# A mixture-of-experts kernel on one core: first expert's rows by one-hot weights, a short main list, and an overflow list made by GpSimd

## What is computed

```python
logits = h @ w_router + b_router                # 512 x 32
top_val, top_idx = top_k(logits, 4)
gates = softmax(top_val)
order = argsort(top_idx.reshape(-1)); tok = order // 4
xs = h[tok]                                     # rows sorted by expert
hgu = ragged_dot(xs, w_gate_up, group_sizes) + b_gate_up[e_sorted]
act = clamped_swiglu(hgu)
out = ragged_dot(act, w_down, group_sizes) + b_down[e_sorted]
moe = segment_sum(out * gates[order], tok)
h = layernorm(ALPHA * h + moe)
```

## Time and profile before

| what | value |
|---|---|
| median of 3 runs | 2309.36 us (2308.25 to 2310.8) |
| the profiled execution | 2309.27 us |
| its span | 2307.4 us |
| mean granted clock of TensorE | 0.985 |
| busy: TensorE, VectorE, ScalarE, GpSimd | 2228.9, 1664.4, 1220.2, 339.9 us |

### The profile page before, as it was taken

The page is one execution under the profiler, slowest core; times in us unless marked ns, Lnnn a source line. Parts: engine busy times, 40 slices in busy tenths (PEclk is TensorE's granted clock), DMA queues, the critical chain, the costliest instruction groups (busy, mean ns, idle before and its releaser), DMA issues.

```text
span 2307.4 us, 29229 instructions
## 1 busy us (share of the span) xinstructions
PE 2228.9 (97%) x10480; PEld 1821.2 (79%) x10480; DVE 1664.4 (72%) x1618; ACT 1220.2 (53%) x1228; POOL 339.9 (15%) x274
## 2 busy tenths in 40 slices
PE   8999959999999999999999999889999999999998
PEld 4668847888888888888888888778777778888886
DVE  2647678999999999999999999882557536433434
ACT  2135336767767777677677777643435532322320
POOL 4042111311111211111112111100130010000000
PEclk9999959999999999999999999999999999999999
DMA  7030149999999999999999999862221232223220
GB/s 276 3 103 1 58 162 357 397 393 381 379 392 377 392 378 379 394 373 386 387 379 393 379 378 396 302 238 83 84 86 37 110 119 100 84 99 110 77 105 37
DMA packets 141524, 551.96 MB, mean 239 GB/s; under 512 B 11552, under 2 KB 12704, under 8 KB 124368
## 3 DMA queue, kind: packets, MB, share of 16 engines
q1 hardware_dynamic: 128240, 507.29, 57.1%
q0 software_dynamic: 10736, 38.93, 6.5%
q10 hardware_dynamic: 2480, 4.80, 0.6%
HBM read 523.18 MB, written 25.69 MB: 238 GB/s over the span
## 4 chain that ended last, share of the span: by engine, by line
PE 79%; DVE 4%; issue 1%; ACT 1%; DMA 0%; DVEq 0%; ACTq 0%
PE PS L389 76%; PE PS L706 1%; PE PS L700 1%; ACT act L1732 1%; DVE ring_parts L2321 1%; DVE small L2408 1%; DVE act L1849 0%; DVE st L1822 0%; PE PS L979 0%; DVE act L1854 0%; DVE act L2435 0%; DMA act<-h_d,tl_c 0%; DVE act L2425 0%; PE PS L880 0%; DVE act L2519 0%
## 5 line engine op out<-in xcount | busy, mean ns | idle before, releaser
L389 PE MATMUL PS<-act_parts 128*128 128x512 f32 x3404 | 1073.2, 394 | 17.3 <-DVE act_parts L2189 8.1
L2034 DVE TENSOR_TENSOR low<-ring,act_parts 128x2048 fp32r<-128x2048 f32 x380 | 851.1, 2293 | 32.6 <-ACT act_parts L1492 32.5
L389 PEld LDWEIGHTS PS<-act_parts 128*128 128x128 f32 x3404 | 641.1, 190 | 150.6 <-issue 17.8
L1492 ACT ACTIVATE act_parts<-ring 128x2048 fp32r<-128x2048 f32 x384 | 707.7, 1914 | 16.4 <-PE PS L389 7.9
L389 PE MATMUL PS<-low,act_parts 128*128 128x512 f32 x1584 | 618.7, 391 | 0.0
L389 PE MATMUL PS<-act_parts,ring_parts 128*128 128x512 f32 (+1 forms) x1344 | 397.1, 382 | 0.0
L389 PEld LDWEIGHTS PS<-low,act_parts 128*128 128x128 f32 x1584 | 298.6, 189 | 60.6
L389 PEld LDWEIGHTS PS<-act_parts,ring_parts 128*128 128x128 f32 x1344 | 248.1, 188 | 58.6 <-issue 10.7
L389 PE MATMUL PS<-ring_parts,act_parts 128*128 128x512 f32 x1088 | 261.7, 393 | 3.1 <-DVE act_parts L2485 2.1
L389 PE MATMUL PS<-ring_parts 128*128 128x512 f32 (+1 forms) x672 | 255.5, 380 | 0.0
L389 PEld LDWEIGHTS PS<-ring_parts,act_parts 128*128 128x128 f32 x1088 | 204.9, 189 | 49.1 <-issue 3.5
(11 more groups left out here) (264 smaller groups left out, 1707.1 us busy)
## 6 DMA issues: line engine op xcount, KB each, us to landing
ring<-w_gate_up SPq DMA_DIRECT2D x264, 1024.0 KB, 8.7
ring<-w_down SPq DMA_DIRECT2D x132, 1024.0 KB, 7.9
ring<-w_ff SPq DMA_DIRECT2D x16, 2048.0 KB, 7.8
ring<-w_in SPq DMA_DIRECT2D x12, 2048.0 KB, 8.1
ring<-w_o SPq DMA_DIRECT2D x1, 4096.0 KB, 24.2
ring<-w_out SPq DMA_DIRECT2D x2, 2048.0 KB, 7.7
acc_d<-ring POOLq DMA_DIRECT2D x5, 512.0 KB, 3.2
act<-x SPq DMA_DIRECT2D x4, 512.0 KB, 5.7
```

The source lines that it names most:

```text
L389: return eng.matmul(o, lhsT, rhs, start=first, stop=last, **kw)
L1492: A_(W1hi[c % CS], W1[c], ACT.Copy).then_inc(sem["high"], 1)
L2034: tt(W1lo[c], W1[c], W1hi[c % CS].bitcast(F32), ALU.subtract).then_inc(sem["low"], 1)
```

## The change

1. **First expert's rows.** As soon as the rank matrix of a token tile is there (now one bank each), VectorE copies it and compares the rank in expert 0 with 0 to 127: a one-hot `OH0`. TensorE multiplies it as weights with h, which lies in SBUF, eight fp32 products of 512 columns (`first_rows`); ScalarE copies the two banks to where a gather would have put the rows. There is no gather for item 0, and item 1's is the first.
2. **Main list.** Only ranks below 128 count, so the list needs no positions: one-hots of the rank, and a table of 64 columns (token number by ScalarE, `token_hot`; gate by VectorE), 16 fp32 products 128x64. It names the tiles of experts 0 to 30.
3. **Overflow.** What is beyond, and the last expert, go to a list of 17 columns. GpSimd makes it while the first items run: counts, prefixes (`count_past`), picks by one-hot (`pick`, twice), and four tables (`over_table`), one for each token tile, of 12 operations. TensorE multiplies them in items 2 and 3, behind chunk 6, two tables each (`list_over`), and VectorE writes the two halves out at the end of items 2 and 3 (`halve_over`, `list_over`), the counts in item 1 (`name_over`).
4. **First gate-up** (`first_gate_up`): bias at its second half first and at the end of the first; the base products two behind each of the chunks 4 to 7, in two banks; the split of gates and down bias by ScalarE and GpSimd. Gate sums by VectorE from the table of the list. Items 1 to 3 are written out, the loop starts at 4.
5. **Order elsewhere.** ScalarE makes three chunks' high parts ahead of the row copies and the others behind; the memset of the bias rows waits for the one-hots; (0,10) and (0,11) are loaded behind item 1's eight chunks; `chunk_low(1, 0)` stands ahead of the last two bases.

The diff, cut to what the steps speak of:

```diff
+            def first_rows(hf):
+                take(hf, "rows_out", hf + 1)
+                for t in range(NT):
+                    if hf == 0:
+                        eng.wait_ge(*past("first_hot", 2 * t + 2))
+                    ins = mm(PS[:, hf, :], OH0[:, t, :], H1[:, t, hf * 512:(hf + 1) * 512], t == 0, t == NT - 1)
+                    if hf == 0 and t == 0:
+                        ranks(3)
+                ins.then_inc(put("rows_psum", hf), 1)
...
+            def list_over(t):
+                eng.wait_ge(*past("over_made", t + 1))
+                for j in range(TOPK):
+                    ins = mm(PS[:, 4, 0:2 * OVER], over_hot[t % 2][:, j, :], over_tok[t % 2][:, j, :],
+                             t % 2 + j == 0, t % 2 + j == TOPK)
...
-            eng.wait_ge(sem["rows_in"], 16)
-            turn_rows()
...
+                        if isinstance(i, int) and i > 1 and c == 6:
+                            eng.wait_ge(sem["down_free"], i)
+                            list_over(2 * i - 4)
+                            list_over(2 * i - 3)
...
+            first_gate_up()
             turn_gated(0, 0)
             turn_gated(0, 1)
-            with eng.Fori(1, LAST) as i:
+            gate_up(1)
+            for b in (4, 5):
+                eng.wait_ge(*free[b])
+            down(1)
+            gate_up(2)
+            eng.wait_ge(*past("over_halved", 1))
+            down(2)
+            gate_up(3)
+            eng.wait_ge(*past("over_summed", 1))
+            down(3)
+            with eng.Fori(4, LAST) as i:
...
+            def first_hot(t):
+                eng.wait_ge(*past("rank_psum", t + 1))
+                eng.tensor_copy(R2[:, t, :], bank_of("rank_psum", t + 1)[:, 0:E]).then_inc(
+                    signal("first_hot"), 1)
+                eng.wait_ge(*latest("first_hot"))
+                ts(OH0[:, t, :], iotas, R2[:, t, 0:1], Mm[:, t, 0:1], ALU.is_equal, ALU.mult).then_inc(
+                    signal("first_hot"), 1)
...
+            for c in range(4, 6):
                 chunk_low(0, c)
             swiglu(0, 0, again=False)
-            for n in range(4, 2 * NT):
+            chunk_low(0, 6)
+            base(0)
+            base(1)
+            chunk_low(0, 7)
+            for n in range(2, 6):
                 base(n)
...
+            chunk_low(1, 0)
+            base(6)
+            base(7)
             swiglu(0, 1, again=False)
             rows_low(1)
-            with eng.Fori(1, LAST) as i:
+            item(1, name_over)
+            item(2, halve_over)
+            item(3, list_over)
+            with eng.Fori(4, LAST) as i:
                 item(i)
...
+            def pick(x, to):
+
+                for t in range(NT):
+                    chosen = slice(TOPK * t, TOPK * (t + 1))
+                    tt(picked[:, chosen, :], OH[:, chosen, :], x[:, t:t + 1, :].to_broadcast([P, TOPK, E]),
+                       ALU.mult).then_inc(signal("pool_step"), 1)
+                eng.wait_ge(*latest("pool_step"))
+                n = E // 2
+                while n > 1:
+                    tt(picked[:, :, 0:n], picked[:, :, 0:n], picked[:, :, n:2 * n], ALU.add).then_inc(
+                        signal("pool_step"), 1)
...
+            def over_table(t):
+
+                if t > 1:
+                    eng.wait_ge(*past("over_psum", t - 1))
+                hot, tok = over_hot[t % 2], over_tok[t % 2]
+                for k in range(TOPK):
+                    n = TOPK * t + k
+                    ts(hot[:, k, :], iotas, slotf[:, n:n + 1], None, ALU.is_equal).then_inc(signal("pool_step"), 1)
+                    ts(tok[:, k, 0:OVER], iotas[:, LAST:ITEMS + 1], itemf[:, n:n + 1], TOKID1[:, t:t + 1],
+                       ALU.is_equal, ALU.mult).then_inc(signal("pool_step"), 1)
...
+            pick(beyond, itemf)
+            next_select(1)
+            pick(more_past, slotf)
+            over_table(0)
+            eng.wait_ge(*past("places_listed", 1))
             eng.wait_ge(*past("sums_begun", 80))
-            with eng.Fori(2, LAST) as i:
+            next_rows(2)
+            add_product(2)
+            over_table(1)
+            next_select(2)
+            over_table(2)
+            next_rows(3)
+            add_product(3)
+            over_table(3)
+            next_select(3)
+            eng.wait_ge(*past("over_listed", 3))
+            with eng.Fori(4, LAST) as i:
                 item(i)
```

More of the change, by code:

```diff
@@ L652, in _ @@
+            ranks(0)
+            cur[0] = 0
             turn_tile(NT - 1)
-            ranks(0)
+            ranks(1)
             router(NT - 1)
-            ranks(1)
             ranks(2)
-            ranks(3)
-            for t in range(NT):
-                ins = mm(PS[0:E, rank_bank, 256:257], Mm[:, t, :], ones[:, 0:1], t == 0, t == NT - 1)
-            ins.then_inc(put("rank_psum", rank_bank), 1)
-            eng.wait_ge(*past("extras", 2))
-            b = next_bank()
-            eng.wait_ge(*free[b])
@@ L730, in base, with bias @@
                     eng.wait_ge(*past("bd_low", 1))
-                if n >= 4:
-                    eng.wait_ge(*past("based", n - 3))
-                b = (4, 5, 2, 3, 4, 5, 6, 7)[n]
+                b = 4 + n % 2
+                take(b, "based", n + 1)
                 mm(PS[:, b, :], GT[:, t, :], bd3[:, hf * 512:(hf + 1) * 512]).then_inc(put("base_psum", b), 1)
-            def gate_up(i, again=True):
-                if not again:
-                    for n in range(4):
-                        base(n)
+            def bias(hh, first):
+                for n in range(2):
+                    cols = slice((2 * hh + n) * 512, (2 * hh + n + 1) * 512)
+                    ins = mm(PS[:, 2 * hh + n, :], sel, bias2[:, cols], first, not first)
+                return ins
@@ new lines, in first_gate_up @@
+            def first_gate_up():
+                for b in range(4):
+                    eng.wait_ge(*free[b])
+                eng.wait_ge(sem["xT_low"], 1)
+                for c in range(8):
+                    hh = c // 4
+                    if c == 4:
+                        eng.wait_ge(*past("bias_lo", 2))
+                        bias(1, True)
+                    eng.wait_ge(sem["low"], count_high(0, c))
+                    for kk in range(2):
+                        k = 2 * (c % 4) + kk
+                        ins = bf3(2 * hh, (xThi[:, k, :], xTlo[:, k, :]), c, kk, hh == 0 and k == 0, hh == 1 and k == KD - 1)
+                    if c == 3:
+                        eng.wait_ge(sem["sel_ready"], 1)
+                        eng.wait_ge(*past("bias_lo", 1))
+                        eng.wait_ge(*past("bias_padded", 1))
+                        ins = bias(0, False)
+                    ins.then_inc(sem["gate_up_used"], 1)
+                    if c == 0:
+                        prefixes()
+                    if c == 3:
+                        turn_gates()
+                    if c >= 4:
+                        base(2 * c - 8)
+                        base(2 * c - 7)
+                eng.wait_ge(sem["rows_in"], 16)
+                turn_rows()
@@ L1555, in item @@
             def item(i, second=False):
-                chunk_high(i, 0)
+                if not second:
+                    chunk_high(i, 0)
                 chunk_high(i, 1)
@@ L2252, in item @@
+            eng.wait_ge(*past("list_psum", 1))
+            ts(tl_i[:, 0:LAST], bank_of("list_psum", 1)[:, 0:LAST], -1.0, 0.0, ALU.add, ALU.max).then_inc(
+                signal("tokens_listed"), 1)
+            for c in range(1, 4):
+                chunk_low(0, c)
+            list_items()
+            def item(i, then=None):
+                if then is not name_over:
+                    chunk_low(i, 0)
                 chunk_low(i, 1)
```

511 lines of the change are left out of this document (268 added, 243 removed).

## The result

| | kernel before | changed kernel |
|---|---|---|
| median | 2310.08 us (4 runs) | 2324.83 us (2322.79 to 2325.12, 4 runs) |
| ratio, 95% interval | | 1.006 (1.0047 to 1.0073) |
| the profiled execution, its span | 2309.27, 2307.4 us | 2322.79, 2320.9 us |
| mean granted clock | 0.985 | 0.986 |

The change makes the kernel 0.6% slower. The forecast was 2312.4 with 2294 to 2323; the median lies 1.8 us above the range. The direction is the forecast's, the size about five times its +3.1.

What follows compares the result with a forecast made beforehand. TensorE, busy 97%, was taken as the bound, with the routing the one place to win. Terms -16.2 + 3.2 + 3.8 + 7.6 + 4.7 = +3.1 on 2309.27 gave 2312.4 us, range 2294 to 2323.

Steps and rivals of the forecast that it cites:

- The start: Routing up to turn_rows(1): turn_rows(0) at 318.9, the clock rising within the eight products, turn_rows(1) at 350.8, gain 16.2 us.
- The waits for tables: TensorE waits for GpSimd's overflow tables, held up beside chunk_low: +7.6 us in item 2, +4.7 in item 3.
- 424.1: Time in us when GpSimd's table 1 is ready, with one GpSimd operation passing after each of 22 chunk_lows.
- 359.2: Time in us when the accumulator's DMA issues end on GpSimd, from which the work up to table 1 was counted.
- the bounds: Limits on GpSimd's delay: below, no exclusion; above, VectorE runs out of chunk_lows at about 423, up to +9.4 us.
- VectorE's lag: Up to rows_low(2), 14 GpSimd operations between VectorE's own cost 4.9 us against 1.6 spare: +3.2 us before item 2's gate-up.
- 1.6 to spare: In a steady item of 35.51 us VectorE is busy 33.91, so it has 1.6 us of room.
- The first (no wait): Rival: exclusion hits only the first operation of a burst, so the tables are in time; 2295 us, chance 0.28.
- The second: Rival: VectorE and GpSimd bound three items, with both tables late to the bound; 2316 to 2322 us, chance 0.15.
- The third: Rival: the start is shortened less, the clock staying at 0.50 until the first gate-up; 2320 us, chance 0.12.
- The lists: Eight small fp32 overflow products in each of items 2 and 3 on TensorE: +3.8 us together.

Runs made afterwards that it cites:

- clock_filler: The changed kernel with 50 matmuls into unused columns between the two halves of each overflow list, where TensorE waits; 2317.10 us.
- few_ops: The changed kernel with each overflow table made by 6 GpSimd operations over all four choices at once instead of 12; 2312.39 us.
- name_early: The changed kernel with VectorE reading the extra counts ahead of chunk_low(1, 8) instead of behind chunk_low(1, 11); 2321.08 us.
- late_early: lists_late with VectorE reading the extra counts and lists early, and TensorE's list products behind chunk 5; 2303.03 us.
- tables_on_vector: The changed kernel with early readings, list products behind chunk 5, and VectorE making the four tables with four operations each; 2297.49 us.
- unread_tables: tables_on_vector with GpSimd also making the changed kernel's four 12-operation tables, which nobody reads; 2306.67 us.
- rows_first: tables_on_vector with rows_low(1) ahead of item 0's second swiglu, and gate_up(1) begun ahead of the second half of item 0's transposes; 2298.31 us.
- few_ops_early: few_ops with the early readings and the list products behind chunk 5; 2303.56 us.
- both: tables_on_vector with the edits of rows_first and busy_before_ranks together; 2296.22 us.
- busy_before_ranks: tables_on_vector with 20 unread filler matmuls in TensorE's wait ahead of the routing's last transposes and 6 behind them; 2293.39 us.
- lists_late: The changed kernel with TensorE's overflow lists in items 3 and 4 instead of 2 and 3, and GpSimd's tables 2 and 3 later; 2311.89 us.

## Why the prediction was wrong

**The start** was right in mechanism and size. turn_rows(0) at 318.97 against 318.9; the clock rose in the middle of the eight products (0.77 in the window 310 to 320), as chosen; turn_rows(1) at 349.85 against 350.8, so the gain is 17.2 and not 16.2.

**The step that failed is the one that isn't there: what TensorE's clock costs behind a wait.** The sum counted waits as their length. Behind each of the four waits of 3.6 us and more the following matmuls ran at the lower clock: worked out from the rows, item by item against the same stretch at the full clock, 1.6 us in item 1 (behind 4.21), 1.6 behind the 3.62, 3.4 and 2.2 behind the two of 6.37, 8.8 in all. clock_filler takes away the last two and gives 5.6 back; the first two are read from rows and no run takes them away alone. The kernel before had such a row, 7.5 us idle at the end of its loop, with three matmuls in 1.62 us behind it that elsewhere take 0.84; I didn't carry it over to new waits. With 8.8 the sum is +11.9, 2321.2, against the profiled 2322.79. Term by term the profile has 17.2 won, and lost 1.05 for rows_low(1) (a wait of 4.21 where the kernel before had 3.16; the forecast took this stretch "as before"), 3.6 for a bank, 12.7 for the tables, 3.6 for the lists and 8.8 for the clock: +12.6 of the measured +13.5.

**The waits for tables** were right in their cause and their sum: 6.37 and 6.37, where 7.6 and 4.7 stood. The parts were not, and that table 1 came within 2.5 us of the 424.1 is partly luck. A 128x17 operation is 0.44 bare and not 0.18, and some waited through two chunk_lows (5.17, 4.50), so it is not one operation behind each; GpSimd also stood idle 4.38 us for TensorE and 4.03 for ScalarE, which no term had. Against that it began 2.5 us sooner than 359.2, and table 0 met a chunk_low in two operations only (2.59 and 2.56). What ended both waits stood in the bounds: VectorE ran out of chunk_lows at 423.50, where the bounds said 423, and GpSimd then ran free. few_ops shows that the count of operations weighs more than their bare work, name_early that the table follows TensorE's pace by about half, through the end of VectorE's row.

**VectorE's lag, 3.2 us, did not come as a wait for low rows.** VectorE did lose time beside the picks: its rows of chunk_low in item 1 took some 2 us more than bare, 10.10 against 8.89 in the row shown under name_early. But late_early and tables_on_vector have the same picks and no wait of TensorE for VectorE behind rows_low(1), and unread_tables none with 48 more operations on GpSimd. 33.91 busy of 35.51 was read as "1.6 to spare"; the likely reason why it did not matter, argued from these runs, is that VectorE runs ahead of TensorE by some chunks. Only rows_first, where TensorE has less to wait elsewhere, finds that store used up.

**A bank was missed.** In its place stood 3.62 us ahead of down(1) for the bank of the extra counts. The code had this wait in so many words, and VectorE's order had the read behind four chunk_lows; that it added about what the lag had is mostly chance. Up to 2 of the 3.62 may be VectorE's lost time, since the read stands behind those chunk_lows; no run separates the two.

**The rivals.** The first (no wait) was wrong for this kernel. The second came nearest by its number, 2316 to 2322, but is not what happened: the scatter-adds issued in 3.53 us and not in 10, TensorE waited 6.37 for each pair of tables and not 9 or more, and late_early and tables_on_vector show that VectorE was not the bound. It left out the clock like the forecast. The third did not happen; its terms add up to 9.3, which would be 2321.7 and not 2320.

**The lists** were 1.8 in an item and not 1.9 (37.33 less 35.51).

## What to carry to other kernels

A wait on the engine that sets the pace costs its length, and in this kernel often 1.6 to 3.4 us of slow matmuls behind it; count both. Work put on an idle engine is not free where its operations are held up beside a busy one (here 0.44 us alone and up to 5.17 beside VectorE's): count operations and not their bare time, and look for when the busy engine's row ends, who waits for the result and what queues behind it. Four operations on the busy engine beat twelve on the idle one, by 2.0 us in the four items even against the best order of the latter (3 us more of the 5.5 in the medians are late_early's idle time at the end of the loop, whose cause is open); and a read that frees a bank belongs ahead of long work, not behind it.

## What the runs showed of the hardware that I had not expected

The length of a wait alone does not tell whether the granted clock falls. In the kernel before TensorE stood 3.16 us at 371 and went on at 1.00; in rows_first it stood 2.46 at 353.83 and went on at 1.00, and 1.97 at 389.36, and about 1 us later its matmuls were 0.43 apart, the lower level. In few_ops it fell behind both waits of 2.21, in few_ops_early behind the one of 1.45 and not behind the one of 1.47. In the profile of `both` it fell in the window 300 to 310 with no wait in it, with the same instructions as busy_before_ranks up to there.

GpSimd's operations beside a row of chunk_low do not pass one after each: a 128x17 took 0.44, 2.21, 4.50 and 5.17 in one table. VectorE pays too, but less: four chunk_lows took 10.10 beside the second pick and 8.99 and 8.89 beside table 1, where the kernel before has 8.89.

The idle time at the end of the loop was 7.5 to 7.6 us in 12 of the 14 profiles, both kernels' among them, and 10.54 in lists_late and late_early; its cause was looked for in one run and not found.
